# Turning the second half of the normalised x in VectorE blocks and scattered stores instead of TensorE transposes, in a one-core fp32 decoder step

## What is computed

```
h    = rmsnorm(x, g_norm)                       # x: 2048 x 1024
proj = einsum('bld,de->ble', h, w_in)           # w_in: 1024 x 10240
u_p, z_p, q, k, v, z_r, gates = split(proj)
...  pooling branch, retention branch, branch projections, gates ...
out  = rmsnorm(x + merged @ w_out, g_final)
```

## Time and profile before

| what | us |
|---|---|
| three runs | 2833.3, 2841.2, 3100.54 |
| median | 2841.2 |
| the profiled execution | 2833.37 |
| its span, first to last instruction | 2831.6 |

### The profile page before, as it was taken

One profiled execution on the slowest core, in us unless ns is written; L12 is line 12 of the kernel. 1 busy time (PEld: TensorE's weight loads), 2 busy tenths in 40 slices (PEclk: granted clock), 3 DMA queues, 4 the chain that ended last, 5 costly groups with the idle time before them and its releaser, 6 DMA issues.

```text
span 2831.6 us, 36714 instructions
## 1 busy us (share of the span) xinstructions
PE 2782.2 (98%) x13504; PEld 2249.1 (79%) x13504; DVE 1808.3 (64%) x2588; ACT 1126.4 (40%) x1901; POOL 684.8 (24%) x456
## 2 busy tenths in 40 slices
PE   6999999999999999999999999999999999999998
PEld 5888888888877777777777787877887888788876
DVE  8667566667555365655755566676677667766775
ACT  5444444444554444443434433333333333333332
POOL 5253433434332223425334330000000000000000
PEclk9999999999999999999999999999999999999999
DMA  4544444454564344453444458487648764876496
GB/s 144 197 146 155 173 147 158 156 179 145 180 223 153 113 156 162 147 186 125 163 154 154 165 200 307 141 278 289 246 145 283 289 239 150 283 290 234 153 340 261
DMA packets 281849, 552.80 MB, mean 195 GB/s; under 512 B 24216, under 2 KB 166872, under 8 KB 270527
## 3 DMA queue, kind: packets, MB, share of 16 engines
q1 hardware_dynamic: 266279, 541.73, 53.5%
q10 hardware_dynamic: 15168, 8.46, 1.0%
q0 software_dynamic: 224, 0.26, 0.0%
HBM read 375.59 MB, written 175.14 MB: 194 GB/s over the span
## 4 chain that ended last, share of the span: by engine, by line
PE 90%; DVE 4%; DMA 2%; issue 2%; ACT 1%; POOL 0%; ACTq 0%; SPq 0%; DVEq 0%; POOLq 0%
PE bank L1310 28%; PE bank L1312 28%; PE bank L1311 28%; PE bank L1360 2%; PE bank L1383 1%; PE bank L1502 1%; DMA raw<-in_w_branch_ret 1%; DVE w_lo L2173 1%; DVE xa_lo L2173 1%; DVE xs L2187 1%; PE bank L1632 1%; PE bank L1620 0%; PE bank L1610 0%; DMA x_d<-x_out 0%; DMA raw<-in_w_branch_pool 0%
## 5 line engine op out<-in xcount | busy, mean ns | idle before, releaser
L1310 PE MATMUL bank<-xa_hi,wa_hi 128*128 128x512 f32 x2240 | 888.8, 397 | 5.5 <-ACT part_s L1864 3.2
L1312 PE MATMUL bank<-xa_hi,wa_lo 128*128 128x512 f32 x2240 | 873.6, 390 | 0.0
L1311 PE MATMUL bank<-xa_lo,wa_hi 128*128 128x512 f32 x2240 | 873.5, 390 | 0.0
L1310 PEld LDWEIGHTS bank<-xa_hi,wa_hi 128*128 128x128 f32 x2240 | 420.6, 188 | 107.8 <-issue 21.5
L1312 PEld LDWEIGHTS bank<-xa_hi,wa_lo 128*128 128x128 f32 x2240 | 420.5, 188 | 90.0
L1311 PEld LDWEIGHTS bank<-xa_lo,wa_hi 128*128 128x128 f32 x2240 | 421.1, 188 | 82.8
L2173 DVE TENSOR_TENSOR wa_lo<-w_raw,wa_hi 128x512 fp32r<-128x512 f32 x320 | 312.7, 978 | 165.9 <-ACT wa_hi L1857 165.1
L2173 DVE TENSOR_TENSOR wa_lo<-w_sum,wa_hi 128x512 fp32r<-128x512 f32 x240 | 194.2, 809 | 241.3 <-ACT wa_hi L1857 241.3
L2173 DVE TENSOR_TENSOR w_lo<-raw,w_hi 128x512 fp32r<-128x512 f32 (+1 forms) x288 | 181.9, 659 | 189.3 <-ACT w_hi L1971 189.2
L1857 ACT ACTIVATE wa_hi<-w_raw 128x512 fp32r<-128x512 f32 x320 | 201.2, 629 | 242.6 <-PE bank L1312 238.3
L1971 ACT ACTIVATE w_hi<-raw 128x512 fp32r<-128x512 f32 (+1 forms) x288 | 166.4, 603 | 306.6 <-PE bank L1312 208.5
(11 more groups left out here) (253 smaller groups left out, 4311.8 us busy)
## 6 DMA issues: line engine op xcount, KB each, us to landing
w_raw<-in_w_in SPq DMA_DIRECT2D x80, 1024.0 KB, 5.3
v_d<-turned SPq DMA_DIRECT2D x64, 512.0 KB, 3.2
qk_s<-qk_d SPq DMA_DIRECT2D x32, 1024.0 KB, 7.4
v_s<-v_d SPq DMA_DIRECT2D x32, 1024.0 KB, 11.5
raw<-in_w_branch_ret SPq DMA_DIRECT2D x128, 256.0 KB, 4.2
tabs<-in_c_rope SPq DMA_DIRECT2D x16, 1024.0 KB, 6.9
qk_d<-high SPq DMA_DIRECT2D x32, 512.0 KB, 4.6
qk_d<-c_low SPq DMA_DIRECT2D x32, 512.0 KB, 5.4
```

Source lines behind the costliest of these rows:

```text
L1310: pe.matmul(out, lh, rh, start=first, stop=False, skip_group_check=onto)
L1311: pe.matmul(out, lh, rl, start=False, stop=False, skip_group_check=onto)
L1312: return pe.matmul(out, ll, rh, start=False, stop=last, skip_group_check=onto)
```

## The change

The second half's x is no longer turned by TensorE. After `x_normalize`, VectorE transposes the pair's tile in place in 32 by 32 blocks (`x_turn_blocks`, four instructions of 128x512, before `x_sums`, which then works on the turned blocks). What is left of the turn is to put the blocks in their places, and that the stores do: SP issues four transfers an operand (`x_store`), each from 32 partitions of the operand, in runs of 32 elements, 128 bytes, 512 runs a transfer. The scratch `x_d` changes its layout to `[PROD, KH, P, T]`, so the read-back has runs of 2048 bytes, 512 an operand. The transposes, the seven `x_copy` a pair and their transfers go. Where `x_rows` and ScalarE's `squares` of the next pair waited for "all seven turned", they now wait for "all 28 transfers landed", since the stores read `xs[0]` and `xq` themselves. The work of a pair is placed one product earlier at its end (`SPREAD`).

```
-SPREAD = (0, 1, 1, 2, 3, 3, 4)
+SPREAD = (0, 0, 1, 1, 2, 2, 3)
+XB = 32
+XA = P // XB
...
-        x_d = scratch("x_d", [PROD, P, KH, T])
+        x_d = scratch("x_d", [PROD, KH, P, T])
...
+            elif n < PAIRS:
+                engine.wait_ge(x_normed, 2 * n + 2)
             else:
-                engine.wait_ge(x_normed, 2 * n + 2)
+                engine.wait_ge(x_blocks, 4 * (n - PAIRS) + 4)
+        def x_pair_stored(engine, n):
+            engine.wait_ge(x_stored, 16 * XA * PROD * (n - PAIRS + 1))
...  SP
             def x_rows(n):
-                if n >= PAIRS:
-                    sp.wait_ge(x_turned, PROD * n)
                 if n == PAIRS:
+                    sp.wait_ge(x_turned, PROD * PAIRS)
                     tab_free(sp, NJ - 1)
+                if n > PAIRS:
+                    x_pair_stored(sp, n - 1)
...
+            def x_store(n, i):
+                x_operand_ready(sp, n, i)
+                for a in range(XA):
+                    t = (n - PAIRS) * P + a * XB
+                    sp.dma_start(x_d[i][:, :, t:t + XB].rearrange("k (b r) t -> r (k b) t", b=XA),
+                                  x_operand(n, i)[a * XB:(a + 1) * XB, :].rearrange("r (b t) -> r b t", t=XB))\
+                        .then_inc(x_stored, 16)
...
             def x_load(i):
                 if i == 0:
-                    for k in range(4):
-                        sp.wait_ge(x_stored[k], 16 * PROD)
-                    sp.wait_ge(x_turned, PROD * NS * PAIRS)
+                    x_pair_stored(sp, 2 * PAIRS - 1)
...
-                sp.dma_start(x_new[i % 3][:], x_d[i]).then_inc(x_new_in[i % 3], 16)
+                sp.dma_start(x_new[i % 3][:], x_d[i].rearrange("k p t -> p k t")).then_inc(x_new_in[i % 3], 16)
...
                 for i in range(PROD):
+                    for k in range(PROD):
+                        n = step(j, i, 5 + SPREAD[k])
+                        if n is not None:
+                            x_store(n, BESIDE[k])
...  GpSimd, VectorE: x_sums
-                pool.wait_ge(x_normed, 2 * n + 2)
+                x_operand_ready(pool, n, A11B11)
...
-                dve.wait_ge(x_normed, 2 * n + 2)
+                x_operand_ready(dve, n, A11B11)
...  TensorE
-                    pe.wait_ge(x_copied, PROD * PAIRS)
...
-                    for k in range(PROD):
-                        n = step(j, i, 5 + SPREAD[k])
-                        if n is not None:
-...
-                            x_transposes(n, BESIDE[k], 6 + m % 2)
...  ScalarE
             def squares(n):
-                    act.wait_ge(x_turned, PROD * (last + 1))
+                    x_pair_stored(act, last)
...
-            def x_copy(n, k):
-...
...  VectorE
+            def x_turn_blocks(n):
+                buf = x_place(n)[0]
+                dve.wait_ge(x_normed, 2 * n + 2)
+                for t in range(2):
+                    for half in range(2):
+                        own = xs[buf][:, t, half * 512:(half + 1) * 512]
+                        dve.transpose(own, own).then_inc(x_blocks, 1)
...
-                    for offset, work in ((2, x_variance), (3, x_normalize), (4, x_sums)):
+                    for offset, work in ((2, x_variance), (3, x_normalize), (4, x_turn_blocks), (4, x_sums)):
```

More of the change, by code:

```diff
@@ L482, in build @@
         x_squared, x_var_ready, x_pow = sem("x_squared"), sem("x_var_ready"), sem("x_pow")
-        x_stored, x_new_in = [sem(f"x_stored{i}") for i in range(4)], [sem(f"x_new_in{i}") for i in range(3)]
-        x_normed, x_turned, x_copied = sem("x_normed"), sem("x_turned"), sem("x_copied")
+        x_stored, x_new_in = sem("x_stored"), [sem(f"x_new_in{i}") for i in range(3)]
+        x_normed, x_turned, x_blocks = sem("x_normed"), sem("x_turned"), sem("x_blocks")
         x_s_dve, x_s_pool, x_hi_done, x_lo_done = sem("x_s_dve"), sem("x_s_pool"), sem("x_hi_done"), sem("x_lo_done")
@@ L1952, in _ @@
                         squares(n)
[L1953 to L1956, removed]
                     if j == NJ - 1 and i:
```

## The result

The changed kernel takes 2855.5 us (median of 5 runs, 2853.6 to 2859.3). Beside runs of the kernel before on the same chip the ratio is 1.007, 95% interval 1.0058 to 1.0081: slower by some 20 us. I forecast 2838, which is 3 us under the shown median of 2841.2; the measured time is inside my range, but against that median the direction was wrong, and so was the size. (In later runs the kernel before had medians of 2834.7 to 2835.9.)

The account below looks back on a forecast made before the run. TensorE, 98% busy, was taken as the bound; its saved 14.3 us would turn into waits for ScalarE, with 5.0 us more: 2833.4 + 5.0 = 2838.4 us on the profiled execution, forecast as 2838, range 2821 to 2893.

Parts of the forecast that it names:

- between: Forecast of 2838 us, set between 2838.4 on the profiled execution's time and the shown median, 7.8 us above that execution.
- the chain: Each pair's squares, blocks turned, stores, load of next x, next squares; claimed to issue the read-back 5.0 us later.
- blocks ended to next load: SP's 28 stores a pair, until all landed: 17.5 us in pairs 4 and 6, 20 in 5 and 7.
- squares to blocks ended: From ScalarE's squares to VectorE's turned blocks: between 8.8 and 13.8 us, taken as 10.
- load of x: SP's load of the next pair's x, after the stores landed and before the next squares: 6.9 us.
- Issue, 0.52 us each: SP's issue of each new store: 0.52 us, so 28 take 14.6 us and end after the packets' 12.5.
- VectorE as the bound: Rival given nothing: VectorE is 64% busy, and the blocks' 2.8 us a pair fit into its lead.
- The packet price, 14 ns: 128-byte store packets on the DMA engines: 14 ns each, by the line through two queues; 12.5 us a pair.
- rivals of dear packets: Stores' 128-byte writes end after the issues: at 30 ns 2890 us (within 2%, 0.24); at 60 ns near 3000 (over 2%, 0.15).
- free stores: Rival, chance 0.13: issue 0.32 us, packet 10 ns or less, so TensorE keeps its 14.3 us: 2819.
- should cost what it did: Read-back of the second half's x: its shorter runs of 2048 bytes were to add no cost.
- The gain, at most 14.3: TensorE's 28 groups of transposes, 12.5 us, plus a 1.8 us wait for normalised x: at most 14.3 us, 0.5%.

Follow-up runs that it names:

- blocks aside: Kernel before plus VectorE's four block transposes a pair, written aside so TensorE's transposes don't wait for them: 2840.3 us, ratio 1.0017.
- 10 apart: Changed kernel with a second x buffer, next x loaded ahead of the stores, squares to PSUM, pairs 10 products apart, not 11: 2831.7 us, ratio 0.9988.
- blocks in the way: Kernel before plus VectorE's four block transposes a pair, in place, TensorE's transposes kept and waiting behind them: 2852.2 us, ratio 1.0063.

## Why the prediction was wrong

The mechanism was the one I had named: SP's issues outlast the packets, the next x waits for them, ScalarE waits for x at the squares, `part_s` and `part_v` stand behind, and TensorE's saved time turns into waits. In its own terms the sum even had the direction right: 2833.4 + 5.0 us on the profiled execution, slower. It read as faster only beside the shown median, which lay 7.8 us above that execution; the later medians of 2834.7 to 2835.9 say that this base was too high, and "between" was a choice, not a reading. What failed is the size of the chain, by a factor of nearly four: I gave it +5.0 us at the read-back, and it was +18.4. Term by term:

| term | predicted | measured | difference |
|---|---|---|---|
| blocks ended to next load, four pairs | 17.5, 20, 17.5, 20 | 18.7, 24.0, 17.2, 23.8 | +8.8 |
| squares to blocks ended, pairs 5 to 7 | 10, 10, 10 | 11.5, 15.4, 12.1 | +9.0 |
| load of x, three times | 6.9 | 5.1, 5.1, 5.5 | -5.1 |
| blocks of pair 4 ended | 704.7 | 705.2 | +0.5 |

- **Issue, 0.52 us each.** The median was right (0.51), but the mean was 0.61 in pair 4, 0.56 in pair 6 and 0.65 over all 112: single issues took up to 3.0 us. A sum of 28 goes by the mean, and I had multiplied a typical value. After the last issue I gave 3 us for the landing and it was 1.5, which hid the error in pairs 4 and 6. In pairs 5 and 7 I had priced the weights between the stores by their bytes, 5.8 us shared with packets; but I added them to the packets (12.5 + 5.8 + 2) where they add to the issues: three more of them, and slower stores after them (12 in 11.47 us), with the engines full for some of it (share 1.00 from 753 to 757 us).
- **Squares to blocks, 10 us.** This is, narrowly, the step that failed most (+9.0 us, beside +8.8 of the stores), "once the squares are late, most places in VectorE's order have come up". The timelines of pair 6 show another thing, a relay across three engines, each late because it had stood behind the squares:

```profile
772.31 0.61 ACT L1850 ACTIVATE wa_hi<-w_raw 128x512 fp32r<-128x512 f32 x1
772.96 0.69 DVE L2162 TENSOR_TENSOR wa_lo<-w_raw,wa_hi 128x512 fp32r<-128x512 f32 x1 [13.60 <-ACT wa_hi L1850]
773.57 0.16 DVE L2169 TENSOR_SCALAR x_var<-x_sum 128x2 f32<-128x2 f32 x1
773.81 0.70 POOL L1197 TENSOR_TENSOR x_inv<-x_var,half 128x2 f32<-128x2 f32 x1 [22.39 <-DVE x_var L2169]
774.46 1.28 POOL L1237 TENSOR_TENSOR w_sum<-w_raw,w_sum 128x512 f32<-128x512 f32 x1
775.83 0.63 ACT L1850 ACTIVATE wa_hi<-w_sum 128x512 fp32r<-128x512 f32 x1 [1.81 <-POOL w_sum L1237]
776.50 1.03 DVE L2162 TENSOR_TENSOR wa_lo<-w_sum,wa_hi 128x512 fp32r<-128x512 f32 x1 [2.77 <-ACT wa_hi L1850]
777.46 3.50 DVE L2176 SCALAR_TENSOR_TENSOR xs<-xs,x_inv,norm_b 128x1024 f32<-128x1024 f32 x2
```

  VectorE had waited 13.6 us and GpSimd 22.4 (the idle times in brackets). `x_inv` was there at 774.5, but the normalisation stood behind a low part, that behind a high part of ScalarE, that behind a sum of GpSimd, which had waited for `x_var`. I had named what is queued behind ScalarE's wait for TensorE's sake (`part_s`, `part_v`), and not that the weights' high parts are queued there too and lead back to the chain.
- **VectorE as the bound, nothing.** Wrong by some 4 us: in the old order the blocks alone cost 3.9 us at the mark, in the changed kernel an eviction behind them holds TensorE for 2.8. I took the mean busy share and a lead of six products for slack at every place.
- **The load, 6.9 us.** 5.1 to 5.5. I had taken the median of all eight loads of x; the three in this stretch had landed in 5.3, 5.7 and 7.0 us in the kernel before already. That the rest comes from an emptier queue was not tried.
- **The packet price, 14 ns.** 13.0 measured. The line through the two queues' means held a factor of four below its lower point, and the read-modify-write that the Trainium skill ("DMA: Bandwidth & Descriptors", Specifications) gives for transfers under 512 bytes was not to be seen in the time of a packet: one of 512 bytes had cost 30 ns, so a shorter one cost less and not more. That it is below line rate, as the same row says, does agree: 128 bytes in 13.0 ns on 16 engines are some 158 GB/s, and the old queue's 558 in 30 ns are 298 (estimates worked out from these prices). The rivals of dear packets fall, at 30 ns and at 60. The free stores fall by the 0.51 us of an issue.
- **The read-back "should cost what it did".** By its layout it did, within 0.8 us a landing; in the changed kernel its median landing was 3.0 us longer. From 18.4 us at its issue to 19.5 at the mark, all that followed added 1.1 us.
- **The gain, at most 14.3.** The transposes were worth their 12.5 us only as far as nobody was due right after them. With the chain undone it was 3 to 5 us, the rest going to the next waits: the read-back, then VectorE's evictions, and, by the sum above, which no run tests, the clock after a wait.
- What I had not foreseen at all is the clock; in the changed kernel taking half of its slow matmuls away moved the mark by 0.8 us.

## What to carry to other kernels

Before you replace one big transfer by many small ones, multiply their number by the mean time of an issue, not by its median, and compare that with the time of their packets: here 28 issues of 0.61 us outlasted 11.6 us of 128-byte packets, and a buffer that they read from stayed locked all that time. When an in-order engine gets a wait, list everything queued behind it and follow each item through the other engines until it either ends or comes back to the chain; the item that comes back is the dear one. And time taken off the bounding engine is worth only the distance to the next thing that is due; find that thing in the timeline (here the landing of the read-back) before you count the gain.

## What the hardware showed that I had not expected

- A transfer of SP's to DRAM, issued back to back, takes 0.45 us with 128 or 256 runs (median) and 0.51 us with 512, with single ones up to 3.0 us; the number of runs is nearly free, the number of transfers isn't. The mean is higher, 0.65 us over the changed kernel's 112 stores, since some of them stood beside a job's weights.
- Writes of 128 bytes to DRAM, scattered, took 13.0 ns a packet on each of 16 engines, 119 to 120 GB/s at a share of 0.76. With two issuing engines it was 141 to 146 GB/s from 712 to 720 us, at a share of 1.08 and 1.01, with the median issue of a sum's store up from 0.51 to 0.89 us.
- In the changed kernel TensorE went on at 1.2 GHz for a few us after waits of 3.6 to 8.0 us, matmuls 0.43 us apart, and at the full 2.4 GHz after waits of 1.1, 1.6 and 2.8 us. In other kernels of this study it fell after 2.0 us (blocks aside), 2.3 us (10 apart) and 2.7 us (blocks in the way) as well, so the length of the one wait doesn't decide it alone.
